# Two transformer blocks on one core: the table written in parts, the scale units and several waits moved, and the second attention's scores and maximum in two VectorE instructions

## The reference, cut to what matters

```
x = first_block(x, c, ...)     # AdaLN, 8 heads of causal attention beside a 31-tap convolution, out projection, SwiGLU
x = second_block(x, c_2, ctx_2, ...)  # AdaLN, 16 heads over 256 latent and 256 context keys, out projection, conv FFN

# attention of the first block (one block of 256 keys)
s = where(k_pos <= q_pos, (q @ k.T) * scale, NEG_INF);  p = softmax(s);  out = p @ v
# attention of the second block
s_lat = (q @ k.T) * scale + bias          # bias by head from a table rpb, masked to a window
s_ctx = (q @ kc.T) * scale
p = softmax(concatenate([s_lat, s_ctx]));  out = p @ [v; vc]
# around them
x = x + g1 * rms_norm(attention_and_conv @ w_out);  h = rms_norm(x) * (1 + sc2) + sh2
x = x + g2 * rms_norm((silu(h @ w_gate) * (h @ w_up)) @ w_down)
```

## Time and profile before

| | us |
|---|---|
| median of 3 runs | 2639.77 |
| lowest and highest | 2638.45, 2647.67 |
| the profiled execution | 2638.73 |
| its span (first to last instruction) | 2637.0 |
| PE busy | 2571.4 |
| DVE busy | 1830.4 |
| ACT busy | 1302.2 |
| POOL busy | 151.8 |

### The profile page before, as it was taken

The page is one execution under the profiler, slowest core; times in us unless marked ns, Lnnn a source line. Parts: engine busy times, 40 slices in busy tenths (PEclk is TensorE's granted clock), DMA queues, the critical chain, the costliest instruction groups (busy, mean ns, idle before and its releaser), DMA issues.

```text
span 2637.0 us, 38198 instructions
## 1 busy us (share of the span) xinstructions
PE 2571.4 (98%) x13356; PEld 2119.6 (80%) x13356; DVE 1830.4 (69%) x2260; ACT 1302.2 (49%) x1860; POOL 151.8 (6%) x258
## 2 busy tenths in 40 slices
PE   7999899999999999999999999999999999999999
PEld 4677787787888888887887878787888888888887
DVE  2349778777897887888756555656588866667565
ACT  2359655534444444465624242425466555555454
POOL 3111111011200000000001010100000000000000
PEclk9999999999999999999999999999999999999999
DMA  9989778589887787788364536453578856656554
GB/s 356 384 323 375 199 271 289 206 317 345 275 300 253 252 269 268 251 308 302 124 216 144 191 96 222 147 190 123 167 250 285 279 177 185 185 169 207 193 192 167
DMA packets 236752, 622.98 MB, mean 236 GB/s; under 512 B 20284, under 2 KB 24679, under 8 KB 231776
## 3 DMA queue, kind: packets, MB, share of 16 engines
q1 hardware_dynamic: 213392, 525.40, 59.4%
q0 software_dynamic: 22448, 91.84, 10.1%
q10 hardware_dynamic: 800, 4.25, 0.4%
HBM read 613.80 MB, written 7.60 MB: 236 GB/s over the span
## 4 chain that ended last, share of the span: by engine, by line
PE 82%; DMA 8%; DVE 5%; ACT 2%; issue 2%; SPq 0%; POOL 0%; DVEq 0%; ACTq 0%
PE ps L2300 12%; PE ps L2241 11%; PE ps L2245 11%; PE ps L2243 11%; PE ps L2697 6%; PE ps L2701 6%; PE ps L2699 6%; PE ps L2302 6%; DMA slot<-in_ada_w 3%; PE ps L2277 2%; PE ps L2281 2%; PE ps L2279 2%; DMA raw<-in_w_down 2%; DVE w_lo L1403 2%; PE ps L2630 1%
## 5 line engine op out<-in xcount | busy, mean ns | idle before, releaser
L1403 DVE TENSOR_TENSOR w_lo<-raw,w_hi 128x1024 fp32r<-128x1024 f32 x762 | 930.0, 1226 | 575.6 <-ACT w_hi L757 573.5
L757 ACT ACTIVATE w_hi<-raw 128x1024 fp32r<-128x1024 f32 x762 | 804.6, 1058 | 982.8 <-PE ps L2245 376.6
L2300 PE MATMUL ps<-h_both,w_hi 128*128 128x512 f32 (+1 forms) x1392 | 485.4, 394 | 2.8 <-DVE h_both L1481 1.7
L2241 PE MATMUL ps<-w_hi,h_both 128*128 128x512 f32 x1152 | 464.4, 403 | 5.1 <-ACT ff L923 2.1
L2245 PE MATMUL ps<-w_hi,h_both 128*128 128x512 f32 x1152 | 450.5, 391 | 0.0
L2243 PE MATMUL ps<-w_lo,h_both 128*128 128x512 f32 x1152 | 450.2, 391 | 0.0
L2302 PE MATMUL ps<-h_both,w_lo 128*128 128x256 f32 (+1 forms) x1392 | 388.5, 279 | 0.0
L2300 PEld LDWEIGHTS ps<-h_both,w_hi 128*128 128x128 f32 x1392 | 261.0, 188 | 63.6 <-DVE h_both L1481 2.4
L1415 DVE SCALAR_TENSOR_TENSOR acc<-ada,cact,acc 128x1024 f32<-128x1024 f32 x224 | 289.2, 1291 | 3.3 <-DMA ada<-in_w_ada 1.7
L2697 PE MATMUL ps<-w_hi,f_hi 128*128 128x512 f32 x680 | 266.1, 391 | 2.4 <-DVE f_lo L1677 1.7
L2699 PE MATMUL ps<-w_lo,f_hi 128*128 128x512 f32 x680 | 265.6, 391 | 0.0
(11 more groups left out here) (283 smaller groups left out, 3164.5 us busy)
## 6 DMA issues: line engine op xcount, KB each, us to landing
ada<-in_w_ada SPq DMA_DIRECT2D x192, 512.0 KB, 4.3
raw<-in_ffn_w_up SPq DMA_DIRECT2D x160, 512.0 KB, 4.5
slot<-in_ada_w POOLq DMA_DIRECT2D x60, 1024.0 KB, 9.5
raw<-in_na_w_qkv SPq DMA_DIRECT2D x96, 512.0 KB, 4.7
raw<-in_w_gate SPq DMA_DIRECT2D x88, 512.0 KB, 5.2
raw<-in_w_up SPq DMA_DIRECT2D x88, 512.0 KB, 4.8
raw<-in_w_down SPq DMA_DIRECT2D x88, 512.0 KB, 5.4
raw<-in_ffn_w_down SPq DMA_DIRECT2D x86, 512.0 KB, 4.4
```

Source lines behind the costliest of these rows:

```text
L757: act.activation(w_hi[:, s, :], raw[:, s, :], ACT.Copy).then_inc(hi_ready, 1)
L1403: dve.tensor_tensor(w_lo[:, s, :], raw[:, s, :], w_hi[:, s, :].bitcast(F32), ALU.subtract).then_inc(lo_ready, 1)
L2241: pe.matmul(o, hi_[:, k, a], wh, start=(k == 0), stop=False)
L2300: pe.matmul(ps[:, 4 * part + g, :].rearrange("p (a n) -> p a n", a=2)[:, :, n], w_hi[:, s, a], h_both[:, :, k, n], start=(k == 0 and ts[-1 ...
```

## The change

- The eight table parts are issued one by one, each behind one more used tile (56 + n), and POOL multiplies `tab` by 1/SCALE first, since the bias is now added before the scaling. A column `zero` is added.
- `max_of` for 512 keys is two fused instructions; the second starts from the minimum of the first. `exp` then has the factor -1 in both blocks. DVE's `qkv2` no longer is a hardware loop for i = 0, 1, but written out.
- Eight scale units stand beside the tight attention, 19 beside tiles 11 to 29.
- PE: beside(0) goes ahead of scores(2); in the first attention v is waited for ahead of values(0) only; the wait for the last `o_used` moves from the end of `attention` to where its banks are written next. ACT: in a tight attention `hi` of one more tile and its stage go ahead of the last out_of; the Sqrt that loads the table goes behind tile 15.
- `out_turn`: rows 0 and 1 go into `last_rows`, ahead of its last step; column sums begin in the pass of t = 1; ACT takes x's statistics of t = 1 ahead of y's of t = 0, rows(0) ahead of y's second ones; DVE makes `diag` ahead of y_gated(0, 0). `boundary`: rows 2 go into the middle of tile 1. Down projection: `last_u` goes behind tile 1.

```diff
@@ POOL @@
+            pool.memset(zero[:, :], 0.0)
...
                     pool.wait_ge(table_landed, 16 * H2)
-                    pool.wait_ge(tile_used, T_AG + RING + 56)
+                    link(pool.tensor_scalar(tab[:, :], tab[:, :], 1.0 / SCALE, None, ALU.mult))
                     for n in range(TABLE_PARTS):
+                        pool.wait_ge(tile_used, T_AG + RING + 56 + n)
                         table_part(n)
@@ scale units @@
-        SC2_LN, SC2_ATT, SC2_OUT = 5, (0, 1, 3, 4, 6, 7), range(11, KD + 16)
+        SC2_LN, SC2_ATT, SC2_OUT = 5, range(PER_GROUP), range(11, KD + 14)
@@ ACT, attention @@
-                    act.activation(prob_of(u, nkt), prob_of(u, nkt), ACT.Exp, scale=-1.0 if nkt == NT else 1.0,
+                    act.activation(prob_of(u, nkt), prob_of(u, nkt), ACT.Exp, scale=-1.0,
...
+                    beside(PER_GROUP)
                     out_of(PER_GROUP - 1)
@@ ACT, out_turn @@
                 x_first(phase, 1)
+                x_stat(n + 1, phase, 1)
                 y_part(phase, 0, Tend)
-                x_stat(n + 1, phase, 1)
+                rows(0)
                 y_stat(n + 2, phase, 0, Tend)
-                rows(0)
@@ ACT, out_rest @@
-                act.activation(stat[:, 61:62], ones[:, 0:1], ACT.Sqrt)
-                for m in range(BESIDE + 1 + PER_GROUP, 2 * KD):
+                for m in range(BESIDE + 2 + PER_GROUP, 2 * KD):
                     out_tile(T0, order, m)
+                    if m == BESIDE + 4 + PER_GROUP:
+                        act.activation(stat[:, 61:62], ones[:, 0:1], ACT.Sqrt)
@@ DVE, max_of @@
+                    least = 3e38
                     if nkt > NT:
-                        dve.tensor_scalar(pr[:, SEQ:2 * SEQ], ps[:, sb, SEQ:2 * SEQ], SCALE, None, ALU.mult)
-                    if nkt == NT:
-                        dve.tensor_tensor_reduce(pr[:, 0:SEQ], ps[:, sb, 0:SEQ], bias[:, b, :], -SCALE, 3e38,
-                                                 ALU.add, ALU.min, stat[:, b:b + 1]).then_inc(max_ready, 1)
-                        return
-                    link(dve.scalar_tensor_tensor(out=pr[:, 0:SEQ], in0=ps[:, sb, 0:SEQ], scalar=SCALE,
-                                                  in1=bias[:, b, :], op0=ALU.mult, op1=ALU.add), off[0])
-                    link(dve.tensor_reduce(stat[:, 2 + b:3 + b], pr, AX, ALU.max), off[0])
-                    dve.tensor_scalar(stat[:, b:b + 1], stat[:, 2 + b:3 + b], -1.0, None, ALU.mult).then_inc(max_ready, 1)
+                        link(dve.tensor_tensor_reduce(pr[:, SEQ:2 * SEQ], ps[:, sb, SEQ:2 * SEQ],
+                                                      zero[:, 0:1].to_broadcast([P, SEQ]), -SCALE, least,
+                                                      ALU.add, ALU.min, stat[:, 2 + b:3 + b]), off[0])
+                        least = stat[:, 2 + b:3 + b]
+                    dve.tensor_tensor_reduce(pr[:, 0:SEQ], ps[:, sb, 0:SEQ], bias[:, b, :], -SCALE, least,
+                                             ALU.add, ALU.min, stat[:, b:b + 1]).then_inc(max_ready, 1)
@@ DVE, out_turn @@
                 lo(Tend, 0)
-                y_gated(phase, 0, 0, bufs[1])
                 scale()
                 make_diag(n + 1, 1)
+                y_gated(phase, 0, 0, bufs[1])
+                rows(0)
+                y_gated(phase, 0, 1, bufs[1])
                 r = rows_rstd(n + 2)
-                y_gated(phase, 0, 1, bufs[1])
-                rows(0)
@@ DVE, second block @@
-            with dve.Fori(0, 2) as i:
-                qkv2(i, True)
+            for i in range(2):
+                qkv2(i)
@@ PE, chunk_tile (through chunk, from qkv2) @@
+                    if j == 0 and o_free is not None and hi_ is hc_hi:
+                        pe.wait_ge(o_used, o_free)
@@ PE, boundary @@
-                tile(1, (1,))
-                more(2)
+                tile(1, (1,), lambda: more(2))
@@ PE, out_turn @@
-                more(0)
-                more(1)
@@ PE, attention @@
                 for u in range(PER_GROUP):
+                    if u == 0:
+                        beside(u)
                     if u + 2 < PER_GROUP and not tight:
                         pe.wait_ge(max_ready, U + (u + 1))
                         scores(u + 2)
-                    beside(u)
+                    if u:
+                        beside(u)
...
+                    if u == 1:
+                        v_there()
                     if u >= 1:
                         values(u - 1)
                 values(PER_GROUP - 1)
-                pe.wait_ge(o_used, U + PER_GROUP)
@@ PE, last_rows @@
-                                             between=iter(()) if t else between)
+                                             between=between if j > 1 or t == 0 else iter(()))
@@ PE, out_rest @@
                     if m == KD:
+                        pe.wait_ge(o_used, units)
...
+            def first_rows(step):
+                if step == RING - 2:
+                    rows(M["x2"], 0, ROWS_TURN, 2)
+                    rows(M["x2"], 1, ROWS_TURN, 2)
@@ PE, down_phase @@
-                    if m == 2:
+                    if m == 1:
                         beside()
```

More of the change, by code:

```diff
@@ L176, in program @@
         pick_c = at("pick_c", [P, 2, 4], S0 + 5696)
-        assert base + S0 + 5728 <= nc.sbuf_usable_end
+        zero = at("zero", [P, 1], S0 + 5728)
+        assert base + S0 + 5760 <= nc.sbuf_usable_end
         ps = ctx.enter_context(nc.psum_tensor("ps", [P, 8, C], F32))
@@ L2222, in bank_free, with chunk_tile @@
                     pe.wait_ge(tr_free[b], m_)
-            def chunk_tile(T, j0, j, targets, width=C, early=False, ts=range(NT), ready=None, between=iter(())):
+            def chunk_tile(T, j0, j, targets, width=C, early=False, ts=range(NT), ready=None, o_free=None, between=iter(())):
                 s = (j0 + j) % RING
@@ L2251, in chunk_tile, with chunk @@
                     mm.then_inc(tile_used, 1)
-            def chunk(T, j0, targets, width=C, middle=None, last=None, rows_ready=None, between=iter(())):
+            def chunk(T, j0, targets, width=C, middle=None, last=None, rows_ready=None, o_free=None, between=iter(())):
                 for j in range(CT):
@@ L2361, in more, with tile @@
                     rows(m_, s_, ROWS_WIDE, xn)
-                def tile(j, ts):
+                def tile(j, ts, halfway=lambda: None):
                     pe.wait_ge(hlo_ready, n0 + rows_done(ROWS_WIDE, j, ts))
-                    wide_tile(T, 0, j, 0, USE0["gate2"], ts=ts, banks_free=y_was_read if ts == (1,) else lambda g: None)
+                    wide_tile(T, 0, j, 0, USE0["gate2"], ts=ts, banks_free=y_was_read if ts == (1,) else lambda g: None,
+                              halfway=halfway)
                 def y_was_read(g):
@@ L2612, in _, with attention @@
             mixer_columns(START_TILES, 1, 1)
-            def attention(U, Mb, nkt, first, beside, tight=False):
+            def attention(U, Mb, nkt, first, beside, tight=False, v_there=lambda: None):
                 def scores(u):
@@ L2673, in conv_mean, with qk_written, v_written, qkv_written @@
                         mm.then_inc(tr_done[0], 1)
-                def qkv_written():
+                def qk_written():
                     pe.wait_ge(pair_free[2], i + (USE2["q1"] + 2))
                     pe.wait_ge(pair_free[0], i + (USE0["k1"] + 2))
+                def v_written():
                     pe.wait_ge(pair_free[1], i + (USE1["v1"] + 2))
+                def qkv_written():
+                    qk_written()
+                    v_written()
                 mixer_columns(T + CT, 0, i + USE0["k1"])
                 for n in range(CT):
+                    if n == 0 and i == 1:
+                        pe.wait_ge(o_used, PER_GROUP)
                     if n == 4:
@@ L2740, in out_first, with out_rest @@
                     out_tile(T0, F0, m, hold if m == 0 else None)
-            def out_rest(T0, F0, m_, first=iter(()), last=iter(()), beside=lambda step: None):
+            def out_rest(T0, F0, m_, units, first=iter(()), last=iter(()), beside=lambda step: None):
                 for m in range(BESIDE + PER_GROUP, 2 * KD - RING):
                     if m == KD:
+                        pe.wait_ge(o_used, units)
                         for b in range(2):
@@ L2764, in second_scale @@
                 yield from column_sums((acc_s,), 5 * UNITS, M["a_sc2"], 4)
-            out_rest(T_OUT1, F_OUT1, M["a_sc2"], last=second_scale())
+            def first_rows(step):
+                if step == RING - 2:
+                    rows(M["x2"], 0, ROWS_TURN, 2)
+                    rows(M["x2"], 1, ROWS_TURN, 2)
+            out_rest(T_OUT1, F_OUT1, M["a_sc2"], UNITS1, last=second_scale(), beside=first_rows)
             out_turn(T_FF1, (*lat, 0, USE0["gate1"]), M["x2"], 2, 8)
@@ L2905, in qkv2 @@
                 both_v = [(*lat, 2, i * 2 + (USE2["qkv2"] + 1)), (*con, 0, i * 2 + (USE0["qkv2"] + 1))]
```

(5 more changed lines are left out.)

18 lines of the change are left out of this document (8 added, 10 removed).

## The result

The changed kernel takes **2616.5 us** (median of 4 executions, 2616.0 to 2617.0) against 2640.2 us for the kernel before (4 executions beside it): ratio 0.9905, 95% interval 0.9886 to 0.9924. The forecast was 2614.8 us, the range 2606 to 2626. Over all executions of this study the medians are 2638.3 us before (57) and 2616.1 us after (10), so the gain is 22 us where the sum of the parts was 24.9.

The account below looks back on a forecast made before the run. PE was taken as the bound, busy 2571.4 of 2637.0 us, leaving 65.6 us idle to win. The terms -8.5, -1.8, -3.0, +0.4, -8.9 and -3.1 sum to -24.9 us, giving 2614.8 us; range 2606 to 2626.

Parts of the forecast that it names:

- the signs that the prediction gave: First attention: no gap over 2 us, tiles landing in 5 to 8 us; later no w_lo wait; PE idle 20 us less.
- 1. First attention: At 279 to 321 us, spreading the table parts removes PE's waits for p: -8.5 us, bounds -1.2 to -9.5.
- Rival A: First attention: the table's load, not its burst, causes the stall, which stays; 7.3 us less gain, 2622.1, chance 0.14.
- The step on the transfers' turns: First attention: by packet-by-packet turns a tile lands quickly beside any burst, so spreading buys nothing; sum 7.3 us smaller.
- 2. End of the tight attention: First block: waits for the last result and o_lo ahead of 425.02 and 429.08 go; -1.8 us, bounds -0.6 to -1.8.
- part 3: End of the first out projection: two scale units less shorten waits for w_lo; -3.0 us, bounds -1.3 to -4.0.
- Part 4: The turn: diag 1.5 us sooner, stalls of 1.9 and some 3.4 us; +0.4 us, bounds -2 to +2.5.
- rival B: The turn: gain of parts 3 and 4 given back, stalls longer and at half clock; 2620.1, chance 0.2.
- 5. Second block: Three attention groups: waits at starts (-5.8 us) and ends (-3.1 us) go; -8.9 us, bounds -3 to -9.5.
- Rivals C and D: Second block: C, p(0) late, 5.8 us less, chance 0.08; D, fused zero-column instruction slow, kernel slower, chance 0.02.
- 6. Small ones: Waits ahead of 1837.46 (-0.7), 1907.40 (-0.9) and 1021.45 (-1.5) shrink; -3.1 us together.

Follow-up runs that it names:

- after_again: The changed kernel itself run once more, unchanged: 2615.4 us (6 executions, 2610.6 to 2626.1).
- before_spread: The kernel before with only the eight table parts spread, each waiting for the tile beside it: 2632.9 us, ratio to before 0.9981.
- beside_late: The changed kernel with the tile of unit 0 behind scores(2) again, the two fused instructions kept: 2618.0 us (4 executions).
- lo_early: The changed kernel with the split of the second turn tile's weights moved forward on ACT and DVE: 2618.0 us (5 executions).

## Why the prediction was right, and where it was off

The forecast was right in sign and, at 1.7 us from the result, in size; PE's idle time fell by 13.9 us, though, where some 20 were expected. The nearness of the total is in part luck. The rows of the table that hold the edits gave 19.4 us in the trace of after against 24.9. Four things that no part of the sum had make up the 21.9: 2.3 us lost before 230 us, 3.8 us won by the pace of the last gate loop, 2.4 us won between 508 and 1011 us, 1.3 us lost between 1024 and 1262 us. Of the signs that the prediction gave, the missing gap, the waits in the turn and scores(2) without a wait came true; tiles landing in 5 to 8 us, no wait for w_lo, and 20 us less idle time did not.

**1. First attention, -8.5: right mechanism, 1 to 2 us too much.** -6.4 and -7.4 measured, -7.0 on average over ten runs with the spread and the early v. The gap went as written, up to the end of the attention (from 3.5 us late to 5.0 us early in the trace after, 8.5 us). Missed was what the parts, now later, do to the columns' slots: PE waits for DMA there, 0.79 us at 337 us, and the stretch from 330 to 342 us (times before) is 0.2 to 1.5 us longer in every trace with the parts spread, 0.1 with the burst. The other 1.2 us between 8.5 and 6.4 lie ahead of the attention, in a wait of 1.12 us for DMA at 260.42 us, before any part is sent. Rival A fell: no wait over 0.73 us in the attention.

The step on the transfers' turns was too simple. In the trace before, the first seven microseconds (283 to 290 us) and then 290 to 300 us show for the two queues (packets, MB, share)

```profile
q0 software_dynamic: 259, 0.82, 96.2%
q1 hardware_dynamic: 13, 0.03, 1.0%
```

```profile
q0 software_dynamic: 443, 1.48, 78.1%
q1 hardware_dynamic: 371, 0.73, 19.3%
```

At first the weights hardly get a packet, though two of their tiles are issued in this window; later they get nearly one for one, but a packet of the table's queue takes over three times as long (0.28 us of an engine against 0.08, from share and count; it carries 3.3 KB against 2.0). The Trainium skill (DMA: Bandwidth & Descriptors, section on queues, rings and completion order) lets the engines take turns packet by packet. The second window agrees with that and the first doesn't, and turns by the packet don't make equal shares of time. The prediction concluded from the rule that a tile would land quickly beside any burst; that doesn't follow. What happens in the first seven microseconds stays open.

**2. End of the tight attention, -1.8:** -1.8 in every run. Right.

**3 and 4. End of the out projection and turn, -3.0 and +0.4.** Together -0.9 on average instead of -2.6. Off is part 3: "two units less are 2.8 us of transfers". PE comes sooner to a stretch that is still full (DMA share 0.97 from 430 to 475 us, 0.99 before). Of the 2.4 us of waits for w_lo at the end 0.5 to 1.6 us stay, and in five of the twelve traces with the change a new one stands at about 450 us (0.24 us in after, 0.37 us in `after_again`). The 1.3 us of half clock counted as won were a matter of the execution: the trace before has two such stretches in the turn, that of `before_spread`, with the same orders there, has one, and of the seven with the new turn six have one and one has two. Part 4 was right in both waits, and its sum of +0.4 is not contradicted. So rival B, gains given back at the turn at half clock, holds by some 1.7 of its 5.3 us, though not by its mechanism of more half clock.

**5. Second block, -8.9:** -6.5 in every run with all its edits. The ends are right (-3.1 predicted; 1.25, 1.04 and 0.61 measured, 2.9). The starts are off: 5.8 predicted, 3.7 measured (1.23, 1.26 and 1.15). The step was "take 0.92 us, so 1.95 us are lost": the two scores last 1.43 us up to the next product of other operands (1378.13 to 1379.56 above) and not 0.92, and scores(2) 0.85 us up to the transposes, where before they lasted 0.56 up to the tile. With the tile in between PE changes operands once more, there and back, and that is the missing 0.7 us a start. Rivals C and D fell: p(0) isn't waited for, and the instruction takes 0.42 us.

**6. Small ones:** -1.7, -0.6 and -0.9 for -1.5, -0.7 and -0.9. Right. For these, and for the 1.2 us of part 2 that are not the wait for the last result, the rows alone speak: only the waits for the last result were put back in a run.

**Not foreseen:** 508 to 1011 us is 2.4 and 3.0 us shorter, of which some 1.5 are waits for w_lo between 574 and 615 us (six before, 2.1 us; two after, 0.7). The row runs from -3.7 to +0.9 over the traces, and between 574 and 615 us the spread alone is 1.5 us shorter too, so most of it is the execution, that of before above all; it was not separated further. From 1024 to 1262 us some 0.5 to 1.3 us are lost to waits for last_f_lo (1.97 us after); its cause wasn't tried either.

## What to carry to other kernels

A wait that has gone is worth its idle time only if no other edit of the same change removes it too and the order of products stays; here one more pair of changes of operands cost some 0.7 us. When a producer's work is thinned out, ask for its last consumer: here two units decided over the column sums and 8 us, several times the 0.8 to 1.9 us by which the waits for w_lo fell. A median of landings over a window that begins ahead of a burst hides it: ask for the transfers beside the burst alone. Before a wait is said to have moved, compare with traces whose clock is the same there. And compare traces stretch by stretch between the same instructions before comparing totals: the clock and a loop's pace moved the totals by more than most parts of the change.

## What the runs showed of the hardware that was not expected

- The pace of an untouched PE loop has two values between executions, 2.77 and 2.83 us a tile (2%), at a granted clock of 1.00 in both, from the first tile of the loop to its last: 3.8 us of the whole. PE never waits in it in either case (busy for all of 180 us from 2160 to 2340 us, 1021 matmul records before and 1041 after). The cause is open.
- Half clock (1.2 instead of 2.4 GHz) comes in stretches of 3.4 to 13.7 us in these traces. It stood behind waits of 1.7 to 3.7 us in the turn, 2.4 to 3.0 us at 86 us, 1.75 us at 140 us and 2.02 us at 597 us (`beside_late`), and once, at 1884 us in `lo_early`, behind waits of 0.51 and 0.66 us that other traces have without it. The Trainium skill (TensorE: Matmul & The Clock Gate, section on HAM oscillation) ties it to idle stretches of PE. These traces agree in that a wait stands ahead of each of these stretches; but 3.03 us of wait were followed by half clock after and not before, so the wait alone doesn't decide. A stretch of 3.4 us costs about 1.5 us.
- One wait of 3.39 us was followed by 13.7 us at half clock, and the stretch was 8.5 us longer than in after: two and a half times the wait.
